# Attention of the later token tiles spread over the expert heads, one tile at a time

## The chip, the cores and the metric

The kernel runs on one core of a Trainium2 chip. The metric is the device time of one execution in microseconds. Engines: TensorE (PE), VectorE (DVE), ScalarE (ACT), GpSimd (POOL) and SyncE (SP). Each runs its own instructions in order and waits for the others on semaphores; 16 DMA engines move data for all of them. SP issues the plain loads and stores, POOL the gathers.

## What is computed

Two transformer blocks over 512 tokens of width 1024, all in float32. The first block (windowed attention with a context, a convolution branch, and a mixture of experts) isn't touched. The second, cut to what matters:

```python
fox_out = forgetting_attention(...)      # 8 heads of 64, causal softmax with a decay
sb_out = stick_breaking_attention(...)   # 8 heads of 64, causal, sigmoids and a reversed cumsum
mixed = concat([rms_norm(fox_out, g_out_fox), rms_norm(sb_out, g_out_sb)], -1)
x = x + gt1 * (mixed @ w_out)                        # w_out: 1024 x 1024, 4 MiB
h2 = rms_norm(x, g_norm_ffn) * (1 + sc2) + sh2
query = (h2 @ w_query).reshape(t, 8, 2, 128)         # w_query: 1024 x 2048, 8 MiB
# peer layer: per head, top 16 of 128 x 128 experts by two halves of the query
u, v = expert_down[experts], expert_up[experts]      # one row of 1024 each
x = x + gt2 * sum(gelu(h2 . u) * gate * v)
return rms_norm(x, g_final)
```

## The kernel before

Tokens are worked in TT = 4 tiles of 128 (P). The second block ends with 32 expert heads, numbered n: head n is expert head n % 8 of token tile n // 8. A head has PARTS = 8 parts, written out by hand on every engine, and each part takes two of the head's 16 expert choices. For a choice, POOL gathers, for the 128 token and expert-slot pairs, a row of 8 KB (the expert's down and up vectors) into one of the pair buffers, 1 MiB in all. VectorE takes the dot product with h2 (`dot`), ScalarE the gelu and scales the gates (`coefs`), TensorE adds the up rows into banks 4 and 5 or 6 and 7 (`up_sums`, one part later). Then the buffer is free and POOL may gather the next choice. Gather m uses buffer m modulo 8 in tile 0 (m < FIRST = 128) and eleven buffers after that: the three others lie in storage that the attention uses until then. In the same parts VectorE finds the top 16 of head n + 2 (`topk_part`).

Before the expert heads, tile 0 alone is attended, and its queries are made. The attention of tiles 1 to 3 (24 units of stick-breaking and 24 of forgetting attention, a unit being one head of one tile, with 256, 384 or 512 keys) is done in steps. Step k of a kind works on unit k and, some steps later, on its follow-up, so the engines have units in flight (`stick_step`, `fox_step`). The first LEAD = 6 steps run ahead of head 0. The others, then the norm (`out_norm`), the turning, the product with w_out in three pairs of blocks, the three `second_norm`s and the first two query heads are dealt out over the first FRONT = 6 expert heads by the table PLAN. In each part the engine does its `peer_part` and then `attend` for the steps of that part. The other six query heads (`query_b`) follow at the ends of heads 6 to 11. Each query head is a product with 256 columns of w_query, loaded by SP as a piece of 1 MiB, for the 384 tokens of all three tiles.

ScalarE has one set of activation functions loaded at a time. `coefs` needs gelu, the attention exp and log, and a switch is an instruction of its own (ACT_TABLE_LOAD).

At a tile's edge h2 is repeated in another order on TensorE and ScalarE (`repeat_rows`, `repeat_out`), the sums of the tile are closed (`edge`), and a tile's final norm (`last_norm`) is made in head 6 of the next tile.

## Time and profile before

| | |
|---|---|
| median of 3 runs | 2968.79 us (2963.34 to 2986.03) |
| profiled execution | 2979.64 us, its span 2977.9 us |
| mean granted TensorE clock | 0.87 |
| busy: TensorE, VectorE, ScalarE, POOL | 2268.4, 1421.2, 759.3, 597.2 us |
| moved by DMA | 922.19 MB, of these 559.01 MB in POOL's queue |

The page gives each engine's busy time, 40 slices of the span, the DMA queues, the chain that ended last, and the costliest groups of instructions. A slice is 74.4 us. The expert heads begin at about 1510 us, in slice 20 counted from 0. Busy times on TensorE and VectorE are of instructions that overlap little or not at all; the share of the DMA engines can be full at 421 GB/s.

### The profile page before, as it was taken

How to read it: one execution, taken by the hardware profiler on the slowest of the kernel's cores; microseconds unless marked ns; L12 is line 12 of the kernel's file. 1: busy time of each engine (PE TensorE's matmuls, PEld its weight loads, DVE VectorE, ACT ScalarE, POOL GpSimd, SP SyncE). 2: the span in 40 equal slices, each digit the busy share in tenths (PEclk: the TensorE clock that was granted, in tenths of full speed). 3: DMA queues.
4: the chain of work that ended last, by engine and by line, in shares of the span. 5: the costliest groups of instructions: out<-in, count | busy, mean ns of one | idle time of the engine just before them, and what ended most of it. 6: DMA issues, size and time to landing. Idle time of an engine off the chain costs nothing. (4 is left out here: it accounts for less than half of the span.)

```text
span 2977.9 us, 28985 instructions
## 1 busy us (share of the span) xinstructions
PE 2268.4 (76%) x9828; PEld 972.8 (33%) x9828; DVE 1421.2 (48%) x3332; ACT 759.3 (25%) x1753; POOL 597.2 (20%) x590
## 2 busy tenths in 40 slices
PE   5997899887777776799988978877765655465554
PEld 2543444432222222655655443322211111111110
DVE  2575401420000001401377667657678777777765
ACT  2104301110000001412177653222222212222212
POOL 0000000010000000000112223344344434344432
PEclk9999999989988988799999889889877777887877
DMA  9268429489999998312347868899999999999996
GB/s 338 60 242 290 164 81 216 189 308 405 400 403 397 396 395 327 114 57 85 138 175 288 305 261 319 361 391 416 417 420 422 421 421 422 420 407 421 422 421 253
DMA packets 211725, 922.19 MB, mean 310 GB/s; under 512 B 18986, under 2 KB 58968, under 8 KB 119694
## 3 DMA queue, kind: packets, MB, share of 16 engines
q0 software_dynamic: 80448, 559.01, 46.3%
q1 hardware_dynamic: 121360, 352.86, 32.4%
q10 hardware_dynamic: 9790, 8.73, 0.9%
q8 instruction: 66, 1.08, 0.1%
q14 instruction: 61, 0.50, 0.0%
HBM read 888.78 MB, written 31.77 MB: 309 GB/s over the span
## 5 line engine op out<-in xcount | busy, mean ns | idle before, releaser
L2604 PE MATMUL bank<-ring,arena_w 128*32 128x512 f32 x1568 | 593.9, 777 | 316.9 <-ACT arena_w L1327 316.6
L894 POOL DMA_INDIRECT ring<-in_expert_pair,ids x392 | 419.4, 1070 | 1037.3 <-PE bank L2604 658.9
L1978 PE MATMUL bank<-arena_h,ring 128*128 128x128 f32 (+2 forms) x1264 | 365.3, 450 | 5.6 <-ACT arena_h L1132 3.2
L2258 PE MATMUL bank<-ring,arena_h 128*64 128x512 f32 x1056 | 278.8, 688 | 85.7 <-DMA ring<-in_w_exp_up 80.8
L2604 PEld LDWEIGHTS bank<-ring,arena_w 128*32 128x32 f32 x1568 | 103.1, 127 | 653.4 <-ACT arena_w L1327 469.3
L1927 DVE CUSTOM_DVE_ANT_0 ring<-ring,arena_h 128x1024 f32<-128x1024 f32 x203 | 245.1, 1225 | 82.2 <-DMA ring<-in_expert_pair,ids 47.4
L1927 DVE CUSTOM_DVE_ANT_0 ring<-ring 128x1024 f32<-128x1024 f32 x189 | 229.6, 1225 | 80.1 <-DMA ring<-in_expert_pair,ids 71.8
L1978 PEld LDWEIGHTS bank<-arena_h,ring 128*128 128x128 f32 x1264 | 206.1, 198 | 155.6 <-issue 119.0
L1325 ACT ACTIVATE arena_w<-arena_w 128x2 f32<-128x2 f32 x256 | 51.9, 203 | 770.7 <-DVE arena_w L1927 770.3
L1650 DVE TENSOR_TENSOR arena_q<-arena_q,bank 128x256 f32<-128x256 f32 x32 | 13.5, 421 | 487.9 <-ACT arena_q L1069 487.9
L2258 PEld LDWEIGHTS bank<-ring,arena_h 128*64 128x64 f32 x1056 | 95.9, 157 | 266.1 <-issue 260.6
L2604 PE MATMUL bank<-arena_h,arena_w 128*32 128x512 f32 x200 | 128.7, 779 | 31.3 <-ACT arena_w L1327 31.3
L1327 ACT ACTIVATE arena_w<-arena_w 128x32 f32<-128x32 f32 x512 | 136.4, 313 | 8.4
L2271 PE MATMUL bank<-ring,arena_q 128*64 128x512 f32 x528 | 120.6, 598 | 19.9 <-DVE arena_q L1653 19.3
L2604 PE MATMUL bank<-pair_last,arena_w 128*32 128x512 f32 x140 | 97.6, 838 | 43.3 <-ACT arena_w L1327 43.3
L2604 PE MATMUL bank<-arena_v,arena_w 128*32 128x512 f32 x140 | 93.4, 804 | 28.6 <-ACT arena_w L1327 28.4
L860 POOL DMA_DIRECT2D ring<-in_w_in x3 | 2.7, 908 | 536.0 <-PE bank L2271 536.0
L1069 ACT ACTIVATE arena_q<-bank 128x256 f32<-128x256 f32 x32 | 12.3, 384 | 327.2 <-PE bank L2258 327.2
L1325 ACT ACT_TABLE_LOAD x63 | 80.8, 1283 | 50.7 <-DVE arena_w L1927 49.9
L1464 DVE SCALAR_TENSOR_TENSOR arena_x<-arena_x,convc 128x512 f32<-128x512 f32 x120 | 90.2, 752 | 4.3
L1984 PE MATMUL bank<-ring,arena_h 128*128 128x512 f32 x192 | 86.4, 606 | 0.0
L1984 PE MATMUL bank<-ring,arena_q 128*128 128x512 f32 x176 | 80.3, 614 | 4.8 <-DVE arena_q L1535 4.8
(473 smaller groups left out, 2982.8 us busy)
## 6 DMA issues: line engine op xcount, KB each, us to landing
ring<-in_w_exp_gate SPq DMA_DIRECT2D x33, 2048.0 KB, 20.2
ring<-in_w_exp_up SPq DMA_DIRECT2D x33, 2048.0 KB, 24.7
...
```

Of the source, the lines that this page charges most:

```text
L894: pool.indirect_dma_start(pair[pair_of(m)], None, A["expert_pair_2"], bass.IndirectOffsetOnAxis(ap=ids[n % 2][:, r:r + 1], axis=0)).then_i ...
L1069: act.activation(silu_g[b], bank[2 + b][:, 0:256], ACT.Silu).then_inc(silu_done, 1)
L1325: link(act.activation(gel[:, k0:k0 + count], dots[:, k0:k0 + count], ACT.Gelu))
L1327: act.activation(sel_q[:, n % 2, k, :], sel_q[:, n % 2, k, :], ACT.Copy, scale=gel[:, k:k + 1]).then_inc(sel_done, 1)
L1464: link(dve.scalar_tensor_tensor(out=conv[:, cc, :], in0=u_pad[:, cc, k:k + T], scalar=convc[:, cc, k:k + 1], in1=conv[:, cc, :], op0=ALU.m ...
L1650: dve.tensor_tensor(hid[b], silu_g[b], bank[2 + b][:, 256:512], ALU.mult).then_inc(hid_done, 1)
L1927: dve.tensor_tensor_reduce(buf, buf, h2_q[r % 4], 1.0, 0.0, ALU.mult, ALU.add, dots[:, r:r + 1]).then_inc(dots_done, 1)
L1978: mm = pe.matmul(dst, w[:, c, at], rhs[:, c, :], start=(c == 0), stop=(c == chunks - 1))
L1984: mm = pe.matmul(dst, xT[:, c, t * P:(t + 1) * P], w[:, c, at], start=(c == 0), stop=(c == chunks - 1))
L2258: mm = pe.matmul(bank[2 + b][at, :].rearrange("p (g f) -> p g f", g=2), xbT[b][:, c, :], gu[:, :, c, 256 * half:256 * half + 256], start=( ...
L2271: mm = pe.matmul(bank[6 + b][CAP * j:CAP * j + CAP, :], hidT[b][:, k, CAP * half:CAP * half + CAP], slab(n)[:, half, k, 512 * j:512 * j + ...
L2604: mm = pe.matmul(bank[4 + 2 * (n // H % 2) + half][at, :], sel_q[:, n % 2, k0 + j, :], pair[pair_of(m + j)][:, D + 512 * half:D + 512 * ha ...
```

## The change

Tiles 1, 2 and 3 are attended one at a time: tile t + 1 during the 8 expert heads of tile t. A plan for a tile (`planned`) deals the 25 attention steps (for tile 1 the 19 that are left after the lead) over the first 30 of the tile's 64 parts, and fixes the parts of the rest: `out_norm` at 30, the turning at 31, the two blocks of w_out at 32 and 36, `second_T` at 39, the eight query heads at 41, 44, 48, 51, 54, 57, 60 and 62. w_out comes in four and w_query in eight pieces of 1 MiB per tile, through the two halves of one buffer (`hold_a`), so both are loaded for each of the three tiles; a query head now multiplies 128 tokens. The shift row of `second_norm` is loaded anew for each tile, since it shares its place with `mixed`. The eight buffers of tile 0 serve until the last tile (FIRST = 384), and the eleven only there. The expert sums always use banks 4 and 5, so the part 1 of a tile waits on TensorE for `last_add` of the tile before. The three final norms move to heads 1, 3 and 5 of the last tile. ScalarE loads the exp and log functions after `coefs` in each part that has an attention step.

The diff, cut to its core:

```diff
...
-        pair += [hold_a[:, 2 * D:4 * D], arena_v[:, 6144:6144 + 2 * D], pair_last[:, :]]
-        FIRST = H * K16
+        pair += [arena_v[:, 2 * D * i:2 * D * i + 2 * D] for i in range(1, 4)]
+        FIRST = (TT - 1) * H * K16
...
-        def wq_b_of(h):
-            if h == 1:
-                return wq_b[1], slab_in[slot2(S_WQ)], loaded2(S_WQ) + 16
-            return wq_b[0], slab_in[slot2(S_FOX + 2)], loaded2(S_FOX + 2) + 16 * max(1, h)
+        PIECES = 4 + H
+        def piece(t, i):
+            at = hold_a[:, 2 * D * (i % 2):2 * D * (i % 2) + 2 * D]
+            turn = 16 * ((t - 1) * PIECES // 2 + i // 2 + 1)
+            there = (slab_in[slot2(S_WQ)], loaded2(S_WQ) + turn) if i % 2 == 0 else (wo_b_in, turn)
+            if i < 4:
+                return at.rearrange("p (c n) -> p c n", c=4), there, cols_cp(A["w_out_2"], i // 2)[:, 4 * (i % 2):4 * (i % 2) + 4, :]
+            h = i - 4
+            return (at.rearrange("p (c n) -> p c n", c=DC), there,
+                    A["w_query_2"][:, h * 2 * P:(h + 1) * 2 * P].rearrange("(p c) n -> p c n", c=DC))
+        def wo_used(t, q):
+            return 2 * TT + 2 + 4 * (t - 1) + q + 1
+        def wq_used(t, h):
+            return 4 + H * (t - 1) + h + 1
...
-            return (n, 0, 0) if n < H else ((n - H) // NT[1], 1 + (n - H) % NT[1], 1)
+            return n % H, n // H, min(1, n // H)
...
-        LAST_AT = 6
+        LAST_AT = (1, 3, 5)
...
-            return first <= n < (H if first == 0 else UNITS)
+            return first <= n < first + H
...
+        ST_FOX = H + OUTS[1]
+        ST_NORM = ST_FOX + H + FOX_OUT[1]
+        ST_TURN, ST_OUT, ST_COLS, ST_QUERY = ST_NORM + 1, ST_NORM + 2, ST_NORM + 4, ST_NORM + 5
         PARTS = 8
         LEAD = 6
-        PLAN = [[[s for s in range(LEAD, STEPS) if int(sum(weight[LEAD:s]) / sum(weight[LEAD:]) * (FRONT * PARTS - 1)) == h * PARTS + p]
-                 for p in range(PARTS)] for h in range(H)]
+        ATTEND_PARTS = 30
+        LATER = {ST_NORM: 30, ST_TURN: 31, ST_OUT: 32, ST_OUT + 1: 36, ST_COLS: 39}
+        LATER.update({ST_QUERY + h: at for h, at in enumerate((41, 44, 48, 51, 54, 57, 60, 62))})
+        def planned(t):
+            first = LEAD if t == 1 else 0
+            plan = [[[] for p in range(PARTS)] for h in range(H)]
+            for k in range(first, ST_NORM):
+                at = (k - first) * ATTEND_PARTS // (ST_NORM - first)
+                plan[at // PARTS][at % PARTS].append(k)
+            for k, at in LATER.items():
+                plan[at // PARTS][at % PARTS].append(k)
+            return plan
+        PLAN = [parts for t in range(1, TT) for parts in planned(t)]
...
-            sp.wait_ge(sbo_pe, UNITS)
-            for j in range(2):
-                sp.dma_start(wo_b[j], cols_cp(A["w_out_2"], j)).then_inc(wo_b_in, 16)
-            sp.wait_ge(o_done, H * TT + UNITS)
-            load_rows(1)
-            for h in range(H):
-                dst, there, _ = wq_b_of(h)
-                if h == 0:
-                    sp.wait_ge(wo_pe, 4 * TT)
-                elif h == 1:
-                    sp.wait_ge(h2_done, 2 * TT)
-                else:
-                    sp.wait_ge(q_pe, 4 + 2 * (h if h > 2 else 1))
-                sp.dma_start(dst, A["w_query_2"][:, h * 2 * P:(h + 1) * 2 * P].rearrange("(p c) n -> p c n", c=DC)).then_inc(there, 16)
-            sp.wait_ge(q_pe, 4 + 2 * H)
-            for dst, src in ((gt2_2, mod2_d[0, 5 * D:6 * D]), (gfin, A["g_final_2"])):
-                sp.dma_start(dst, src.partition_broadcast(P)).then_inc(rows2_in, 16)
+            sp.wait_ge(q_pe, 2)
+            sp.wait_ge(o_done, H * TT + H)
+            load_halves(rows_2[1][0], 2 * D)
+            load_row(rows_2[1][1], mod2_d[0, 4 * D:5 * D])
+            load_row(rows_2[1][3], A["g_norm_ffn_2"])
+            for t in range(1, TT):
+                sp.wait_ge(o_done, H * TT + (t + 1) * H)
+                for i in range(PIECES):
+                    dst, (there, _), src = piece(t, i)
+                    if 2 <= i < 6:
+                        sp.wait_ge(wo_pe, wo_used(t, i - 2))
+                    elif i >= 6:
+                        sp.wait_ge(q_pe, wq_used(t, i - 6))
+                    sp.dma_start(dst, src).then_inc(there, 16)
+                    if i == 1:
+                        sp.wait_ge(attT_pe, 2 * t + 2)
+                        load_row(rows_2[1][2], mod2_d[0, 3 * D:4 * D])
+                        if t == 1:
+                            load_halves(gt2_2, 5 * D)
+            load_row(gfin, A["g_final_2"])
             for t in range(TT):
                 sp.wait_ge(fin_done, t + 1)
...
                         pool.wait_ge(q_pe, m - 1)
                     if m == FIRST:
-                        pool.wait_ge(wo_pe, 4 * TT)
-                        pool.wait_ge(q_pe, 4 + 2 * 2)
-                        pool.wait_ge(qh_done, H)
...
+            def query_out_b(t, h):
+                act.wait_ge(q_pe, wq_used(t, h))
+                link(act.activation(qT2[:, h, :], bank[1 + h % 3][:, 0:2 * P], ACT.Copy), q_done)
+            def attend(t, s):
                 if s < ST_FOX:
-                    stick_step(H + s, H)
+                    if s == 0 and t >= 2:
+                        act.wait_ge(q_pe, wq_used(t - 1, H - 1))
+                    stick_step(H * t + s, H * t)
                 elif s < ST_NORM:
-                    fox_step(H + s - ST_FOX, H)
+                    fox_step(H * t + s - ST_FOX, H * t)
                 elif s == ST_NORM:
-                    out_norm(1)
-                elif s < ST_OUT:
-                    for k in range(DC):
-                        act.wait_ge(attT_pe, 2 + k + 1)
-                        link(act.activation(mixT2[1][:, k, :], bank[(1, 2, 3, 6, 7)[k % 5]][:, 0:3 * P], ACT.Copy,
-                                            scale=gob[:, k // AC:k // AC + 1]), attT_done)
-                elif s < ST_QUERY:
-                    t = s - ST_OUT
-                    if 1 <= t < TT:
-                        second_norm(t, 1, rows_2[1][3])
-                    for u in {4: (1,), 5: (2, 3)}.get(t, ()):
-                        second_columns(u, 1, h2T_2[1][:, :, (u - 1) * P:u * P], H2T_BANKS[u])
-                else:
-                    query_out_b(s - ST_QUERY)
+                    out_norm(t)
+                elif s == ST_TURN:
+                    turned_out(t)
+                elif s == ST_OUT + 1:
+                    second_norm(t, 1, h2r_2[t])
+                elif s == ST_COLS:
+                    second_columns(t, 1, h2T_2[1], H2T_BANKS[1])
+                elif s >= ST_QUERY:
+                    query_out_b(t, s - ST_QUERY)
...
-                if n < H and PLAN[n][part]:
-                    if any(s < ST_FOX for parts in PLAN[n:] for steps in parts for s in steps):
-                        act.preload_act_table_set(EXP_LN)
+                if n < len(PLAN) and any(s < ST_NORM for s in PLAN[n][part]):
+                    act.preload_act_table_set(EXP_LN)
...
-            def attend(s):
+            def attend(t, s):
                 if s < ST_FOX:
-                    stick_step(H + s, H)
+                    stick_step(H * t + s, H * t)
                 elif s < ST_NORM:
-                    fox_step(H + s - ST_FOX, H)
+                    fox_step(H * t + s - ST_FOX, H * t)
                 elif s == ST_NORM:
-                    out_norm(1)
-                elif 1 <= s - ST_OUT < TT:
-                    t = s - ST_OUT
                     if t == 1:
                         norm_gain(1)
-                    second_norm(t, 1, *rows_2[1][0:3], h2r_2[t], tmp_2[1], WO_BANKS[t])
+                    out_norm(t)
+                elif s == ST_OUT + 1:
+                    second_norm(t, 1, *rows_2[1][0:3], h2r_2[t], tmp_2[1], WO_BANKS[1], (rows2_in, 16 * (10 + t)))
...
-            def last_norm(t):
+            def last_add(t):
+                dve.wait_ge(peer_done, t + 1)
                 for j in range(2):
                     at = slice(512 * j, 512 * j + 512)
-                    dve.wait_ge(peer_done, t + 1)
-                    link(dve.tensor_tensor(tmp_p, bank[4 + 2 * (t % 2) + j][:, :], gt2_2[:, at], ALU.mult))
+                    link(dve.tensor_tensor(tmp_p, bank[4 + j][:, :], gt2_2[j], ALU.mult))
                     link(dve.tensor_tensor(xr[:, t, at], xr[:, t, at], tmp_p, ALU.add), fin_add if j == 1 else None)
+            def last_norm(t):
                 one = slice(t, t + 1)
                 dve.wait_ge(ssq_done, SQ_LAST + t + 1)
                 link(dve.tensor_scalar(rms_t[:, one], ssq[:, one], 1.0 / D, EPS, ALU.mult, ALU.add), ms_done)
...
-            def query_b(h, halves=(0, 1)):
-                w, there, count = wq_b_of(h)
-                pe.wait_ge(there, count)
-                for half in halves:
-                    m = 2 * h + half
-                    if m >= 3:
-                        pe.wait_ge(q_done, 4 + m - 2)
-                    project(bank[1 + m % 3][:, 0:3 * P], w, slice(half * P, (half + 1) * P), h2T_2[1]).then_inc(q_pe, 1)
-            def attend(s):
+            def query_b(t, h):
+                w, there, _ = piece(t, 4 + h)
+                pe.wait_ge(*there)
+                if h >= 3:
+                    pe.wait_ge(q_done, wq_used(t, h - 3))
+                for half in range(2):
+                    mm = project(bank[1 + h % 3][:, half * P:(half + 1) * P], w, slice(half * P, (half + 1) * P), h2T_2[1])
+                mm.then_inc(q_pe, 1)
+            def attended_b(t, j):
+                for half in range(2):
+                    w, there, _ = piece(t, 2 * j + half)
+                    pe.wait_ge(*there)
+                    for c in range(4):
+                        mm = pe.matmul(bank[WO_BANKS[1][j]][:, :], mixT2[1][:, 4 * half + c, :], w[:, c, :],
+                                       start=(half == 0 and c == 0), stop=(half == 1 and c == 3))
+                    mm.then_inc(wo_pe, 1)
...
-                    if s == 0:
+                    if s == 0 and t == 1:
                         pe.wait_ge(q_done, 4)
                         pe.wait_ge(proj_out, 18 + PROJS)
-                    stick_step(H + s, H)
+                    if s == 0 and t >= 2:
+                        pe.wait_ge(q_done, wq_used(t - 1, H - 1))
+                        pe.wait_ge(rep_done, 8 * t)
...
-                        second_T(1, 1, h2r_2[1], H2T_BANKS[1])
-                    if t == TT + 1:
-                        pe.wait_ge(res_done, 2 * (TT + 3) + 2)
-                        second_T(2, 1, h2r_2[2], H2T_BANKS[2])
-                    if t == TT + 2:
-                        pe.wait_ge(h2T_done, 2 * (TT + 1) + 2)
-                        second_T(3, 1, h2r_2[3], H2T_BANKS[3])
+                    fox_step(H * t + s - ST_FOX, H * t)
+                elif s == ST_TURN:
+                    turned(t)
+                elif ST_OUT <= s < ST_OUT + 2:
+                    if s == ST_OUT:
+                        pe.wait_ge(attT_done, 2 * t + 2)
+                    attended_b(t, s - ST_OUT)
+                elif s == ST_COLS:
+                    second_T(t, 1, h2r_2[t], H2T_BANKS[1])
                 elif s >= ST_QUERY:
                     if s == ST_QUERY:
-                        pe.wait_ge(h2T_done, 4 * TT)
-                    query_b(s - ST_QUERY)
+                        pe.wait_ge(h2T_done, 2 * (TT + t) + 2)
+                    query_b(t, s - ST_QUERY)
...
+                if part == 1 and n % H == 0 and n > 0:
+                    pe.wait_ge(fin_add, n // H)
+                    edge(True)
                 if part >= 1:
...
             pe.wait_ge(rep_done, 8)
             for s in range(LEAD):
-                attend(s)
+                attend(1, s)
             for n in range(TT * H):
                 t = n // H
                 if n % H == 0 and t > 0:
-                    if t == 1:
-                        pe.wait_ge(q_done, 4 + 2 * (n - FRONT + 2))
+                    pe.wait_ge(q_done, wq_used(t, H - 1))
                     repeat_rows(t, range(3))
                 if n > 0:
                     up_sums(n - 1, K16 - 2, 2)
                 if n % H == 0 and t > 0:
+                    edge(False).then_inc(peer_done, 1)
                     repeat_rows(t, range(3, 8))
-                    edge(t - 1, False).then_inc(peer_done, 1)
-                    if t >= 2:
-                        pe.wait_ge(fin_add, t - 1)
-                    edge(t, True)
                 if n > 0 and n + 2 < TT * H:
                     peer_scores(n + 2)
                 for part in range(PARTS):
                     peer_part(n, part)
-                    for s in PLAN[n][part] if n < H else ():
-                        attend(s)
+                    for s in PLAN[n][part] if n < len(PLAN) else ():
+                        attend(t + 1, s)
                     if n == 0 and part == 0:
                         spread(1)
                         peer_scores(2)
-                if FRONT + AHEAD - 1 <= n + 1 < FRONT + H - 1:
-                    if n == H:
-                        pe.wait_ge(rep_done, 8 * 2)
-                    query_b(n + 1 - FRONT + 1)
             up_sums(TT * H - 1, K16 - 2, 2)
-            edge(TT - 1, False).then_inc(peer_done, 1)
+            edge(False).then_inc(peer_done, 1)
...
```

## Rows read from the trace of the kernel before

**Rows 1.** The page's 40 slices, 74.4 us each: DMA busy tenths, GB/s
```profile
DMA  9268429489999998312347868899999999999996
GB/s 338 60 242 290 164 81 216 189 308 405 400 403 397 396 395 327 114 57 85 138 175 288 305 261 319 361 391 416 417 420 422 421 421 422 420 407 421 422 421 253
```

**Rows 2.** Stretches: PE, PEld, DVE, ACT, POOL busy (count), granted clock, DMA share, GB/s
```profile
1521.00:1957.00 436.00, 371.75 (x1706) 182.21 (x1704) 309.48 (x745) 228.30 (x456) 123.30 (x120) 0.86 0.79 306
1957.00:2300.00 343.00, 228.38 (x1036) 71.58 (x1032) 245.67 (x604) 86.00 (x256) 147.73 (x131) 0.82 1.01 415
2340.00:2920.00 580.00, 333.27 (x1490) 73.73 (x1490) 429.73 (x1032) 135.64 (x424) 246.13 (x231) 0.79 1.01 419
2360.00:2590.00 230.00, 130.09 (x544) 27.85 (x546) 173.99 (x430) 52.63 (x167) 97.32 (x92) 0.79 1.01 421
1521.00:1630.00 109.00, 96.81 (x555) 61.95 (x552) 93.19 (x218) 89.53 (x154) 31.70 (x30) 0.92 0.71 266
```

**Rows 3.** The DMA view, 1900 to 2160 us: queues and query loads
```profile
q0 software_dynamic: 13882, 101.08, 94.1%
q1 hardware_dynamic: 5228, 5.36, 6.2%
...
ring<-in_w_query SPq DMA_DIRECT2D x5, 1024.0 KB, 22.4
```

**Rows 4.** All eight query loads, from issue to landing
```profile
DMA to landing us min/median/max: 6.0/14.9/26.9
```

**Rows 5.** Stretches of 10 us, columns as in rows 2
```profile
1920.00:1930.00 10.00, 10.00 (x58) 4.95 (x59) 6.86 (x15) 1.14 (x4) 4.01 (x4) 0.78 1.01 421
1930.00:1940.00 10.00, 9.14 (x43) 4.06 (x41) 4.15 (x12) 2.25 (x9) 2.03 (x3) 1.00 0.99 375
1940.00:1950.00 10.00, 3.63 (x8) 0.55 (x8) 7.01 (x19) 1.42 (x6) 5.64 (x6) 0.57 0.99 394
...
1990.00:2000.00 10.00, 6.03 (x32) 2.27 (x32) 7.41 (x24) 1.78 (x8) 3.86 (x3) 0.97 0.76 282
```

**Rows 6.** TensorE in order of time: start, duration, what
```profile
1476.57 7.31 PE L1978 MATMUL bank<-arena_h,ring 128*128 128x128 f32 x64
...
1515.26 1.12 PE L2453 MATMUL bank<-ring,later_neg 128*128 128x512 f32 x2 [0.84 <-DVE ring L1738]
...
1517.74 1.00 PE L2469 MATMUL bank<-arena_v,ring 128*128 128x64 f32 x8
...
1520.60 1.91 PE L2604 MATMUL bank<-ring,arena_w 128*32 128x512 f32 x8
1522.44 1.16 PE L2445 MATMUL bank<-arena_v 64*128 64x128 f32 x8
...
1782.14 7.13 PE L1984 MATMUL bank<-arena_v,arena_q 128*128 128x512 f32 x16
```

**Rows 7.** Groups by line and shape, 1510 to 1760 us
```profile
L1188 ACT ACTIVATE ring<-ring,ones 128x512 f32<-128x512 f32 x7 | 5.1, 723 | 0.2
...
L1738 DVE TENSOR_TENSOR ring<-ring,before 128x128 f32<-128x128 f32 x19 | 5.5, 292 | 0.7
...
L1735 DVE SCALAR_TENSOR_TENSOR ring<-bank,ring 128x512 f32<-128x512 f32 x7 | 4.8, 691 | 1.9 <-ACT ring L1188 1.7
...
L1745 DVE TENSOR_TENSOR ring<-bank,ring 128x256 f32<-128x256 f32 x7 | 3.0, 423 | 3.3 <-PE bank L2457 2.9
```

**Rows 8.** ScalarE in order of time
```profile
1869.42 1.28 ACT L1320 ACT_TABLE_LOAD   x1
1870.71 0.21 ACT L1320 ACTIVATE arena_w<-arena_w 128x16 f32<-128x16 f32 x1
```

**Rows 9.** VectorE in order of time: first and last of one second_norm
```profile
1796.52 0.69 DVE L1545 TENSOR_TENSOR ring<-bank,arena_v 128x512 f32<-128x512 f32 x1
...
1804.79 1.23 DVE L1553 TENSOR_TENSOR ring<-ring,arena_v 128x1024 f32<-128x1024 f32 x1
```

**Rows 10.** Waits, 1960 to 2340 us: total, times, longest
```profile
DVE ring L1927 <- ACT arena_h L1334: 20.4, 2, 15.8
```

249 lines of the change are left out of this document (104 added, 145 removed).

## The prediction

> **What bounds the kernel now.** I read the page in slices first, for where the DMA engines are full and where they are not [rows 1]. Slices 20 to 26, counted from 0, move 175 to 391 GB/s; from slice 27 on it is 416 to 422 with one dip, up to the last. So the expert heads of tiles 1 to 3 are bound by the gathers, and those of tile 0, which carry the whole attention of the other three tiles, by something else. Then the busy times by stretch [rows 2]. A gather is 128 rows of 8 KB, 1.049 MB, and at 421 GB/s takes 2.49 us. From 1957 us on the chip keeps to it (231 gathers in 580 us, 2.51 each). Before that, 1521 to 1957 us, 120 gathers take 436 us, 3.63 each, at 306 GB/s, while TensorE is busy 371.8 of 436 us. In the part with stick-breaking attention (1521 to 1630 us) three engines are nearly full: TensorE 96.8, VectorE 93.2, ScalarE 89.5 of 109 us. The reader should see that the time lost is DMA time, 436 x (421 - 306)/421 = 119 us, and that engines lose it. I then went to single instructions for what the engines do per pair of gathers [rows 6, 7], and to the weight loads in the DMA view [rows 3, 4], since the change buys the 119 us with more of these.
>
> **Removed.** The front's excess: at best tile 0 becomes bound by DMA, -119 us. The next two tiles lose in the trace of before 343 x 6/421 = 5 us (415 GB/s instead of 421 [rows 2]); they are rebuilt too, so these go to the credit: -124.
>
> **Added transfers.** w_out (4 MiB) and w_query (8 MiB) are read for each of three tiles instead of once: 24 MiB more, 25.2 MB, at 421 GB/s 60 us. The shift row is read three times instead of once: 1.05 MB, 2.5 us. Query pieces have runs of 1 KB (1025 bytes a packet against 7281 for gathers [rows 3]); in the stretch with five of them the rate is 415. If all of its 5 us were theirs it would be 1 us a piece, if none 0; I take 0.5 for the 24 pieces that the new stretch holds, 12 us (0 to 24). Sum with no stall anywhere: -124 + 60 + 2.5 + 12 = -49 us. As the total is now DMA-bound everywhere, this is the ceiling of the gain; with free query pieces -61.
>
> **What the attention costs inside a DMA-bound head.** A pair of gathers (one part of a head) takes 4.98 us of DMA. Engines need for it, from 2360 to 2590 us (92 gathers, 46 pairs), TensorE 2.8, VectorE 3.8, ScalarE 1.1 us [rows 2]; VectorE's gaps between dependent instructions add some 0.4 (an estimate: a third of its 1.2 us of idle time), 4.2. The plan puts 25 steps (19 for the first tile) in 30 parts. A stick unit of 512 columns costs TensorE 1.16 + 3.48 = 4.6 us at full clock, a pair's sums 1.9 [rows 6]; VectorE three operations of 0.69 and one of 0.3, with gaps 2.5 us; for 256 columns 0.42 each, 1.7 [rows 7]. Eight units take 13 steps, at 1.2 parts a step 15.6 parts: VectorE 4.2 + 8 x 2.5/15.6 = 5.5 us per part for the last tile, 5.3 for the middle one (2.1 a unit), 5.0 for the first. Over 4.98 that is 8 us, 4 us, 0. TensorE stays below: 1.9 + 0.5 x 4.6 = 4.2 at the full 2.4 GHz, 4.9 at the front's granted 0.86 of it (a mean of that level and 1.2 GHz, with the engine busy 85% of the time). Engines that are all near full hold each other up: from 1521 to 1630 us a pair took 7.3 us where the busiest engine had 6.45, 12% more. At lower load I take a third of it over 30 parts, 6 us for each of three tiles (bounds 0 and 18): 18. Sum 30 us.
>
> **The serial steps.** Eight gather buffers hold 20 us of transfers, of which a part in work needs about half. What a stop costs is in the trace: with eight buffers, a query block of 10.6 us on TensorE (in 1920 to 1940 us) left rates of 421, 375 and 394, in sum 1.7 us of DMA [rows 5]. So the new blocks of 7.1 us (attended_b, half of w_out) and 3.7 us (a query head, 7.3 for two [rows 6]) cost nothing in themselves; with the cover gone they would cost themselves, 24 x 3.7 + 6 x 7.1 = 131 us. second_norm is 9.5 us on VectorE's in-order queue [rows 9], and the dots of the next pair, their ScalarE scaling, TensorE's sums and so the next gathers wait behind it; with the wait for TensorE's block some 14 us, 4 beyond the cover. out_norm is shorter. 3 us a tile, 9 (0 to 20). At a tile's edge VectorE waited 15.8 us for the repeated rows and the DMA lost 3.3 us in the worst 10 us [rows 5, 10]; the new edge has no 10.6 us block beside it, but TensorE now waits at part 1 for last_add (banks 4 and 5 are shared), behind which all its sums are queued. I keep 3 us for two edges, 6 (0 to 15).
>
> **Weights that come late.** SP issues a piece only when one of two halves is free, and the query steps stand 3 parts apart (6 gathers and a piece, 7.34 MB, 17.4 us). Under full gathers a piece of 1 MiB landed after 22.4 us, at the least load after 6.0 [rows 3, 4]. TensorE waits in order, sums behind it, gathers behind these. But while it waits the DMA works on gathers and piece alike. At 1.05 MB/22.4 us the piece has 47 GB/s and the gathers 374, for 16.8 us, the piece has 0.79 MB by then, and 0.26 MB at 1.05 MB/6.0 us add 1.5: 18.3 instead of 17.4. At 24 steps 21 us; some steps are 4 parts apart, so I take half, 10 (0 to 34). The arbitration that this rests on is a rule of the Trainium skill too ("DMA: Bandwidth & Descriptors", Queues, rings and completion order): each engine takes whole packets from its queues in turn. By that rule small packets against large ones get a small share, which agrees with the 22.4 us; it speaks against re-reading weights under gathers, and is the mechanism of the second rival.
>
> The w_out pieces are the same case: 0 and 1 are issued when the last fox unit is out (part 28) and wanted at part 32, 20 us later, 2 and 3 wanted 4 parts after the first are used; their runs are 2 KB. They are in the 10.
>
> **Moved for nothing.** sqT and fqT are stored by tile, in copies of the same size. The lead of six steps is all 256 wide: up to 5 us earlier, against as much of ramp; 0. The three final norms come in the last tile, with eleven buffers: 8 output rows' worth of DMA there instead of 4, and one edge; +2. SP's output stores now stand behind all pieces, and nobody waits for them before the end. Behind SP's new wait for the turned rows (attT_pe) stand only the shift row, which VectorE wants five parts later, and pieces that have no free half yet. POOL's one wait at the first gather of tile 3 is for attention that ended a tile's half ago. ScalarE's and TensorE's waits at a tile's first step are for queries that the preceding part has brought.
>
> **Sum.** -49 + 30 + 9 + 6 + 10 + 2 = +8 us; as coinciding stalls hide one another, I take off a tenth of the 55 us of stalls: +3. The profiled execution took 2979.64 us (span 2977.9), 10.9 above the median of three, so a difference is what carries over: 2982.6 beside it, 2968.8 + 3 = 2972 as median.
>
> **Rivals.** First, the gain arrives: the late weights are work for the DMA engines and cost nothing, and the coupling is 0, so 12 + 3 + 3 + 2 = 20 remain of the stalls, and -49 + 20 = -29, or with cheap query pieces -41: 2934. For it: the 10.6 us block that cost 1.7. Against: VectorE alone needs 5.3 to 5.5 us a part in two tiles.
> Second, slower: TensorE's waits for query pieces, parts 41 to 62. If all eight gathers have landed when a piece comes, the DMA engines stand for the 3.7 us block and the first sums (1.9), 5.6 us less what the next piece covers; at 2.5 us on average, 24 steps, +60 - 10 = +53: 3022, and at the full 5.6 +127: 3096. It decides from the point at which a piece lands later than 17.4 us after its slot came free. For it: 22.4 us. Against: the queue is then less full, and 6.0 us were seen. Less than nothing it can't cost: no step starts before its piece.
> Third, the engines' coupling stays at the front's 12% for 30 parts of three tiles (54 us instead of 18): +39, 3008.
> Fourth, ScalarE's table switches. Each part with a step switches to the exp/log set and back, 69 parts, 138 loads of 1.28 us; the load is followed by its activation with no gap (1869.42 + 1.28, next at 1870.71 [rows 8]). In the 15.6 parts of a 512 wide stick stretch ScalarE then has 26 loads (33 us), four activations of some 0.65 us a unit (0.72 the longest [rows 7]; 21 us) and 0.9 a part for the scaling (14 us), 4.4 us a part. If a switch cost twice its 1.28 us it would be 6.5 (6.0 in the narrowest tile), 1.3 above the DMA over 90 parts, 117 us in place of the 30 above: +90, 3059. For it speaks a page only, against it the row. The page is "ScalarE: Activation LUTs" of the Trainium skill, What ACT_TABLE_LOAD costs: it adds a drain of about 1.38 us to each load. By that rule the kernel would be clearly slower; the trace shows no such time.
> Fifth, the change doesn't do what it says: tile 0 stays at over 3 us a gather because the granted clock falls, the new bytes are paid and half of the 119 returns: +60, 3030.
>
> **How the numbers follow.** Forecast, within 1%: 0.44. Gain arrives: 0.26, of which 0.22 beyond 1%. Late weights: 0.14. Coupling: 0.08, half of it beyond 1%. Table switches 0.04, first tile not freed 0.04. So faster by over 1% 0.22; slower 0.14 + 0.04 + 0.04 + 0.04 = 0.26; within 0.52. 1%, 30 us, is about what this kernel's measurement can tell from no change (its three runs span 23 us). The range leaves out the upper half of the late weights, the table switches and the deepest gains: 2925 to 3030.
>
> **What would show it.** Right: from about 1530 us on 405 to 421 GB/s through three tiles; the gather of tile 1's start near 1870 instead of 1957, that of tile 3's start within 20 us of before; VectorE busy 75 to 90% in all three. Dips at the norms and the edges, of under 5 us each. Late weights: waits of TensorE for query DMAs of over 3 us, with the rate under 380 in the second half of each tile. Coupling: rate under 390 in the first half of the second and third. I would be wrong outright if buffers drained at every part, or if the small packets cost much more DMA time than 0.5 us a piece.

## The result and the profile after

| | before | after |
|---|---|---|
| median | 2968.24 us (4 runs) | 3020.2 us (2998.02 to 3037.1, 4 runs) |
| ratio, 95% interval | | 1.0168 [1.0136, 1.02] |
| profiled execution, its span | 2979.64, 2977.9 us | 2998.02, 2996.2 us |
| moved by DMA | 922.19 MB | 948.46 MB |

The change makes the kernel 1.7% slower. The profiled execution after is the fastest of its four, so the two profiles are only 18 us apart. First the page after: slices (as [rows 1]) and the two large queues.

```profile
GB/s 336 59 247 289 155 87 221 183 323 405 406 400 399 399 394 306 85 56 85 190 319 419 388 359 410 292 400 416 387 410 316 388 401 363 411 395 421 422 422 298
...
q0 software_dynamic: 80448, 559.01, 46.1%
q1 hardware_dynamic: 142832, 379.08, 34.6%
```

Slices 20 to 26, counted from 0, rose from 175 to 391 GB/s to 292 to 419, as the change wanted. But slices 28 to 35, full before with one dip, now fall to 316, 363 and 387. The stretches say the same; columns as in [rows 2], and each of the first three is about one tile's heads:

```profile
1500.00:1880.00 380.00, 250.40 (x1246) 105.57 (x1245) 262.78 (x646) 137.57 (x319) 135.10 (x124) 0.80 0.94 379
1880.00:2260.00 380.00, 274.43 (x1446) 121.16 (x1446) 274.73 (x667) 170.46 (x360) 135.01 (x128) 0.85 0.97 381
2260.00:2640.00 380.00, 281.81 (x1511) 130.68 (x1511) 272.34 (x654) 175.00 (x357) 138.27 (x130) 0.87 0.96 379
2640.00:2900.00 260.00, 156.86 (x758) 40.58 (x756) 194.74 (x479) 70.74 (x202) 114.59 (x101) 0.77 1.00 415
```

Three tiles in a row stay at 380 GB/s, no engine above 75% busy: they are bound by DMA, with holes. Where are the holes? Five stretches hold most of them: around the two w_out blocks of tiles 0, 1 and 2, and around the ends of tiles 0 and 1.

```profile
1700.00:1760.00 60.00, 37.59 (x193) 15.94 (x191) 34.57 (x84) 13.63 (x37) 16.61 (x16) 0.83 0.82 315
2100.00:2140.00 40.00, 25.11 (x141) 10.32 (x141) 29.96 (x71) 12.66 (x33) 11.40 (x12) 0.79 0.96 370
2500.00:2540.00 40.00, 29.04 (x172) 13.37 (x172) 30.81 (x76) 10.50 (x33) 15.39 (x15) 0.81 0.84 325
1860.00:1920.00 60.00, 43.55 (x265) 22.06 (x264) 33.28 (x80) 30.50 (x57) 16.94 (x16) 0.91 0.77 296
2240.00:2340.00 100.00, 83.69 (x492) 45.40 (x493) 73.48 (x167) 61.75 (x109) 30.32 (x29) 0.91 0.86 324
```

Against 421 GB/s the three w_out stretches lose 60 x 106/421 + 40 x 51/421 + 40 x 96/421 = 29 us, and the two ends 18 + 23 = 41 us. In a second profile of the same kernel (after_again) the same five stretches carry 356, 357, 364, 334 and 326 GB/s and lose 21 and 35 us, so a single trace gives these sums only roughly. The worst of them, in order of time: SyncE's issues of pieces, and TensorE's w_out blocks in tile 0.

```profile
1646.05 0.94 SPq L786 DMA_DIRECT2D ring<-in_w_out  x2
...
1676.76 3.82 SPq L786 DMA_DIRECT2D ring<-in_w_out  x2
1701.84 13.20 SPq L786 DMA_DIRECT2D ring<-in_w_query  x2
```

```profile
1696.72 5.08 PE L2556 MATMUL bank<-ring 128*128 128x512 f32 x8 [2.79 <-DMA ring<-in_w_out]
1708.39 6.07 PE L2556 MATMUL bank<-ring 128*128 128x512 f32 x8 [6.59 <-DMA ring<-in_w_out]
```

Pieces 2 and 3, issued from 1676.76, are not there at 1701.8, 25 us later. TensorE stands 6.59 us, VectorE's `second_norm` behind it, the dots behind that, and the eight gather buffers stay full. VectorE waits 15.12 us for the second block, and POOL issues no gather for 20.17 us:

```profile
1714.57 0.69 DVE L1558 TENSOR_TENSOR ring<-bank,arena_q 128x512 f32<-128x512 f32 x1 [15.12 <-PE bank L2556]
```

```profile
1717.09 0.94 POOL L919 DMA_INDIRECT ring<-in_expert_pair,ids  x1 [20.17 <-PE bank L2611]
```

From 1700 to 1760 us the chip issues 16 gathers, against 21 in e6_free below, with the same packets. TensorE's waits for pieces in the three tiles:

```profile
PE bank L1994 <- DMA ring<-in_w_query: 36.4, 9, 7.7
PE bank L2556 <- DMA ring<-in_w_out: 16.5, 4, 6.6
```

Nine waits of 24 query steps, and four at w_out: fewer than the prediction's second rival had them, and longer.

### The profile page after: what moved, and what is told of

The parts are those of the page before. It is cut to its first block, busy times and chain, and to the rows that moved or that the text cites. A ratio compares the mean times of both kernels' runs of the same rounds, so it can differ in the third digit from the quotient of the medians.

```text
span 2996.2 us, 30146 instructions
## 1 busy us (share of the span) xinstructions
PE 2276.9 (76%) x10340; PEld 1025.6 (34%) x10340; DVE 1421.4 (47%) x3340; ACT 843.0 (28%) x1824; POOL 603.0 (20%) x590
## 2 busy tenths in 40 slices
DMA packets 233201, 948.46 MB, mean 317 GB/s; under 512 B 19466, under 2 KB 75832, under 8 KB 141166
## 4 chain that ended last, share of the span: by engine, by line
PE 40%; DMA 34%; DVE 16%; issue 5%; ACT 4%; POOL 1%; SPq 0%; another core or an unknown queue 0%; DVEq 0%; ACTq 0%; POOLq 0%
PE bank L1994 16%; DMA ring<-in_w_exp_up 12%; DMA ring<-in_expert_pair,ids 10%; DVE ring L1941 6%; DMA ring<-in_w_query 6%; PE bank L2274 5%; PE bank L2000 5%; PE bank L2611 5%; DMA ring<-in_w_out 2%; DMA arena_h<-in_expert_pair,ids 1%; PE bank L2556 1%; DMA ring<-in_w_mod 1%; PE bank L2013 1%; ACT L1346 1%; DVE arena_h L1941 1%
## 5 line engine op out<-in xcount | busy, mean ns | idle before, releaser
L2611 PE MATMUL bank<-ring,arena_w 128*32 128x512 f32 x1668 | 574.4, 747 | 348.3 <-ACT arena_w L1348 345.3
L919 POOL DMA_INDIRECT ring<-in_expert_pair,ids x417 | 457.5, 1097 | 1131.0 <-PE bank L2611 749.2
L1941 DVE CUSTOM_DVE_ANT_0 ring<-ring,arena_h 128x1024 f32<-128x1024 f32 x232 | 279.4, 1224 | 103.6 <-DMA ring<-in_expert_pair,ids 79.7
L1665 DVE TENSOR_TENSOR arena_q<-arena_q,bank 128x256 f32<-128x256 f32 x32 | 13.5, 421 | 481.0 <-ACT arena_q L1094 481.0
L2611 PE MATMUL bank<-arena_h,arena_w 128*32 128x512 f32 x236 | 142.3, 735 | 13.8 <-ACT arena_w L1348 13.8
L1346 ACT ACT_TABLE_LOAD x94 | 120.6, 1283 | 93.1 <-DVE arena_w L1941 92.2
L1994 PE MATMUL bank<-ring 128*128 128x128 f32 x768 | 115.8, 322 | 36.4 <-DMA ring<-in_w_query 36.4
L2287 PE MATMUL bank<-ring,arena_q 128*64 128x512 f32 x528 | 120.6, 598 | 20.0 <-DVE arena_q L1668 19.4
L1994 PEld LDWEIGHTS bank<-ring 128*128 128x128 f32 x768 | 111.7, 235 | 65.8 <-DMA ring<-in_w_query 51.8
```

Of the source, the lines that this page charges most:

```text
L919: pool.indirect_dma_start(pair[pair_of(m)], None, A["expert_pair_2"], bass.IndirectOffsetOnAxis(ap=ids[n % 2][:, r:r + 1], axis=0)).then_i ...
L1346: link(act.activation(gel[:, k0:k0 + count], dots[:, k0:k0 + count], ACT.Gelu))
L1941: dve.tensor_tensor_reduce(buf, buf, h2_q[r % 4], 1.0, 0.0, ALU.mult, ALU.add, dots[:, r:r + 1]).then_inc(dots_done, 1)
L1994: mm = pe.matmul(dst, w[:, c, at], rhs[:, c, :], start=(c == 0), stop=(c == chunks - 1))
L2287: mm = pe.matmul(bank[6 + b][CAP * j:CAP * j + CAP, :], hidT[b][:, k, CAP * half:CAP * half + CAP], slab(n)[:, half, k, 512 * j:512 * j + ...
L2611: mm = pe.matmul(bank[4 + half][at, :], sel_q[:, n % 2, k0 + j, :], pair[pair_of(m + j)][:, D + 512 * half:D + 512 * half + 512], start=Fa ...
```

## The experiments

The table gives each kernel's median, its ratio to the kernel before on the same chip with its interval, and what it changes. Differences between kernels of different comparisons are taken between ratios.

| kernel | us | ratio [95%] | what |
|---|---|---|---|
| after_again | 3010.89 | 1.0127 [1.009, 1.0164] | the changed kernel |
| e1_cut_pieces | 2895.1 | 0.9712 [0.9663, 0.9761] | pieces of one eighth |
| e2_wide_runs | 2950.05 | 0.9927 [0.9904, 0.995] | same bytes, 8 KB runs |
| e3_narrow | 2994.86 | 1.009 [1.006, 1.0121] | attention 256 wide |
| e4_no_wait | 3008.59 | 1.0111 [1.007, 1.0153] | pieces not waited for until the tile's end |
| e6_free | 2970.64 | 1.0016 [0.999, 1.0042] | the same, and issued early |
| e5_before_eight | 2975.8 | 1.0005 [0.998, 1.0029] | before, eight buffers in tiles 1 and 2 |
| e7_no_gelu | 3000.33 | 1.0107 [1.006, 1.0153] | Gelu replaced |
| c_pairs | 2976.4 | 1.0009 [0.9982, 1.0036] | query pieces in 2 KB runs |
| c_long | 2958.75 | 0.9947 [0.9923, 0.997] | all pieces in 4 KB runs |
| c_shift | 2962.79 | 0.9976 [0.9952, 1.0] | c_long, attention over 34 parts |
| c_mid | 2952.62 | 0.9927 [0.9906, 0.9949] | c_long, attention over 32 parts |

**The changed kernel again.** 

> The changed kernel once more, to see its spread beside the others and to have a second profile. Both theories: 1.01 to 1.02 of before, 2998 to 3037 us.

42 us above before (2969.41): the slowdown is real, 1.3 to 1.7%.

**Pieces: bytes or runs?** e1_cut_pieces (the w_out and w_query products of tiles 1 to 3 are then made of what lay in the buffer):

```diff
-                    sp.dma_start(dst, src).then_inc(there, 16)
+                    at8 = slice(0, 256)
+                    sp.dma_start(dst[:, 0:1, at8], src[:, 0:1, at8]).then_inc(there, 16)
```

> The changed kernel, but each of the 36 weight pieces loads an eighth of its 1 MiB (the rest of the piece is what lay there, so queries and attention output of tiles 1 to 3 are wrong). Every wait stays. 33 MB less are moved, 78 us at 421 GB/s. Theory A (late pieces: the DMA engines stand idle around the steps that wait for a piece): 78 + 12 for small packets + 25 to 40 for lateness, some 115 to 130 us faster than the changed kernel, 2890 to 2905, 0.97 to 0.98 of before. Theory B (the engines' coupling in the attention parts loses the time, lateness nothing): 78 to 90 us faster, 2930 to 2942.

e2_wide_runs loads other rows, whole, into the same halves (so TensorE multiplies with other weights):

```diff
-                    sp.dma_start(dst, src).then_inc(there, 16)
+                    flat = hold_a[:, 2 * D * (i % 2):2 * D * (i % 2) + 2 * D]
+                    if i < 4:
+                        src = A["w_out_2"][256 * i:256 * i + 256, :].rearrange("(p r) n -> p (r n)", r=2)
+                    else:
+                        src = A["w_query_2"][P * (i - 4):P * (i - 3), :]
+                    sp.dma_start(flat, src).then_inc(there, 16)
```

> The changed kernel, each piece still 1 MiB but read in runs of 8 KB instead of 1 or 2 KB (other elements of the same weights, so the numbers of tiles 1 to 3 are wrong). Theory A, with the small share of small packets as the reason for the lateness: a piece lands in 8 to 12 us under full load instead of over 20, 35 to 50 us faster than the changed kernel. Theory B: 5 to 12 us faster, from the packets alone.

The pieces' DMAs from issue to landing, first in the changed kernel (after_again), then with 8 KB runs; the last figure of the longer rows is the median:

```profile
DMA to landing us min/median/max: 7.4/26.9/38.2
ring<-in_w_query SPq DMA_DIRECT2D x24, 1024.0 KB, 29.0
ring<-in_w_out SPq DMA_DIRECT2D x12, 1024.0 KB, 19.0
```

```profile
DMA to landing us min/median/max: 8.7/9.4/13.8
ring<-in_w_query SPq DMA_DIRECT2D x24, 1024.0 KB, 9.3
ring<-in_w_out SPq DMA_DIRECT2D x12, 1024.0 KB, 9.5
```

e1_cut_pieces lies in theory A's range, and e2_wide_runs gains more than its 35 to 50 us. The same megabyte lands in a third of the time, and the kernel gains 61 us (3010.89 - 2950.05). The landing time falls with the length of the runs: 29.0 us with 1 KB, 19.0 with 2 KB, 9.3 and 9.5 with 8 KB. The bytes cost too: e1_cut_pieces moves 33 MB less than e2_wide_runs, 78 us at 421 GB/s, and is 55 us faster (64 by the ratios, give or take 16). But these bytes were in the prediction's sum. What it missed is the shape of the pieces, and that alone turns the gain of e2_wide_runs, 0.7%, into a loss of 1.3%.

**How wide is the attention's share?** e3_narrow gives tiles 2 and 3 the attention of tile 1:

```diff
-            return n % H, n // H, min(1, n // H)
+            return n % H, min(1, n // H), min(1, n // H)
```

> The changed kernel, but the attention of tiles 2 and 3 is that of tile 1, 256 keys wide (its numbers are wrong there); all steps, waits and loads stay. Theory B (three engines near full hold each other up at 384 and 512 keys): 25 to 40 us faster than the changed kernel, no stretch below 400 GB/s in the first half of tiles 1 and 2. Theory A: under 10 us faster.

16 us by the medians, 0.37% (11 us) with 0.48% of uncertainty between the ratios. That meets neither theory's figure and can't be told from nothing: it doesn't show what the width costs.

**Late, or merely small?** Small runs could cost in two ways: TensorE waits, or the queue carries less. In e4_no_wait TensorE multiplies with another resident array; the products of tiles 1 to 3 are left out in effect, the loads stay.

```diff
+                    if i >= 2:
+                        sp.wait_ge(*piece(t, i - 2)[1])
...
-                w, there, _ = piece(t, 4 + h)
-                pe.wait_ge(*there)
+                w = skT[:, 0:DC, :]
+                if h == H - 1:
+                    for i in (PIECES - 2, PIECES - 1):
+                        pe.wait_ge(*piece(t, i)[1])
...
-                    w, there, _ = piece(t, 2 * j + half)
-                    pe.wait_ge(*there)
+                    w = view(arena_w, 0, 4, 512)
```

> The changed kernel with all its 36 pieces loaded as they are (same bytes, same 1 KB and 2 KB runs, nearly the same moments), but TensorE multiplies with another resident array in their place and waits for the pieces only once per tile, before their place in the buffer is used again. It leaves the second block's w_out and w_query products of tiles 1 to 3 out. Theory A (what costs is that the pieces arrive after they are wanted, and everything queued on TensorE, ScalarE and VectorE stands): most of what the long runs gave comes back here too, 2950 to 2970 against 3010.9 for the changed kernel. Rival B (what costs is the queue's lower rate while small packets pass, and the bytes themselves; the waits are covered): within 12 us of the changed kernel, 2999 to 3015.

3008.59: taken alone, this spoke for rival B. The trace says otherwise. Two stretches of e4_no_wait, and a wait of its TensorE (line 1996 is the last query head, which waits for the last two pieces of the tile; the profile names no releaser):

```profile
1720.00:1740.00 20.00, 16.50 (x110) 7.62 (x112) 15.78 (x38) 5.53 (x19) 8.98 (x8) 0.80 1.03 404
1880.00:1900.00 20.00, 18.89 (x146) 7.04 (x144) 10.86 (x26) 11.97 (x23) 4.55 (x5) 1.00 0.56 211
...
```

```profile
PE bank L1996 <- issue: 30.9, 2, 16.5
```

The hole at w_out is gone, but the lateness had only moved to the tile's end: I had left a wait there, and the last piece still came late. So e6_free issues each piece as soon as its half's last one has landed, instead of after its use:

```diff
-                    if 2 <= i < 6:
-                        sp.wait_ge(wo_pe, wo_used(t, i - 2))
-                    elif i >= 6:
-                        sp.wait_ge(q_pe, wq_used(t, i - 6))
+                    if i >= 2:
+                        sp.wait_ge(*piece(t, i - 2)[1])
```

> As e4_no_wait (TensorE multiplies with another resident array, the second block's w_out and w_query products of tiles 1 to 3 are left out), but the queue of the pieces is no longer paced by their use either: each piece is issued as soon as the one before it in its half of the buffer has landed, so that all twelve of a tile are there long before the one wait at its end, where e4_no_wait still stood 14 and 16 us. Same bytes, same 1 KB and 2 KB runs. Theory A (lateness costs): the stalls of the w_out steps and of the tiles' ends are gone, 2950 to 2975 against 3010.9 for the changed kernel. Rival B (small packets lower the rate whether they are waited for or not): 2995 to 3015.

2970.64. The five stretches of before in this kernel, and one more of query pieces:

```profile
1700.00:1760.00 60.00, 36.10 (x220) 14.49 (x220) 42.97 (x100) 16.95 (x45) 23.28 (x21) 0.83 1.03 408
2100.00:2140.00 40.00, 26.27 (x156) 12.55 (x156) 28.97 (x72) 10.29 (x30) 18.61 (x15) 0.84 1.02 411
2500.00:2540.00 40.00, 26.72 (x156) 12.42 (x156) 25.57 (x62) 9.10 (x28) 16.86 (x16) 0.83 1.03 411
1860.00:1920.00 60.00, 50.35 (x276) 24.92 (x271) 47.91 (x109) 43.93 (x78) 19.36 (x19) 0.91 0.84 320
2240.00:2340.00 100.00, 87.11 (x473) 42.26 (x469) 82.74 (x187) 73.71 (x122) 33.05 (x32) 0.93 0.88 340
...
1740.00:1860.00 120.00, 81.23 (x510) 40.92 (x508) 76.54 (x183) 27.73 (x83) 47.79 (x40) 0.87 1.02 410
```

The w_out stretches lose 4 us instead of 29, the ends 14 + 19 = 33 instead of 41. That is 33 us less (19 less when set against after_again's profile). The ratios give 1.0127 - 1.0016 = 1.1%, 33 us (give or take 13). TensorE still waits at the last query head of a tile, but 8.8 us in three times where e4_no_wait had 30.9 in two. What stays of the 61 us, 0.9% or 26 us (give or take 10), is then small packets without lateness. The last row fits that: with small packets passing the DMA engines are full (1.02) and carry 410. The same stretch of e2_wide_runs:

```profile
1740.00:1860.00 120.00, 78.17 (x460) 38.70 (x462) 81.01 (x199) 27.38 (x84) 47.03 (x42) 0.84 1.01 421
```

In the three tiles such packets pass for some 600 us; 600 x 11/421 = 16 of the 26 us, by this estimate. The other 10 are within the error.

**Fewer buffers.** e5_before_eight is the kernel before with this part of the change alone:

```diff
-        FIRST = H * K16
+        FIRST = (TT - 1) * H * K16
```

> The kernel before with one part of the change alone: eight gather buffers until the last tile, where it had eleven from tile 1 on. If the prediction's tiles 1 and 2 are right in holding the queue full (415 to 419 GB/s) with less cover, this costs under 8 us (2965 to 2977 against 2969). Rival: the three buffers fewer, some 8 us of stock less for every stall, are what uncovers the coupling, and cost 15 to 40 us alone (2985 to 3010).

```profile
2340.00:2920.00 580.00, 338.43 (x1492) 72.59 (x1492) 428.25 (x1029) 135.17 (x423) 255.94 (x234) 0.77 1.01 418
1960.00:2300.00 340.00, 223.96 (x985) 68.79 (x983) 241.16 (x589) 84.50 (x250) 136.25 (x125) 0.81 0.99 404
```

Tile 1 carries 404 GB/s, 415 before, and the rest as much as before [rows 2]. The whole costs 1.5 us by the ratio, with an interval of -6 to +9: in the kernel before, the three buffers are not it. Whether eleven would have covered the late pieces in the changed kernel isn't shown; there the attention holds their storage.

**Table switches.** e7_no_gelu replaces the experts' activation by one that needs no table of its own:

```diff
-                link(act.activation(gel[:, k0:k0 + count], dots[:, k0:k0 + count], ACT.Gelu))
+                link(act.activation(gel[:, k0:k0 + count], dots[:, k0:k0 + count], ACT.Square))
```

> The changed kernel with the experts' Gelu replaced by Square, which needs no other table of ScalarE: the 163 table loads of 1.28 us (209 us of ScalarE) go, nearly all. This changes the values of the output, not the work. Fourth rival (table switches lie on the chain dot, coefficient, multiplication, free buffer): 2960 to 2985 against 3010.9. Against it: ScalarE is idle half of every tile and the loads are covered: within 10 us of the changed kernel.

I had the count wrong: the 94 loads ahead of the Gelu went, but the preload of the exp set, 69 times, stayed. The page's groups of after, then of e7_no_gelu:

```profile
L1346 ACT ACT_TABLE_LOAD x94 | 120.6, 1283 | 93.1 <-DVE arena_w L1941 92.2
...
L1367 ACT ACT_TABLE_LOAD x69 | 88.5, 1283 | 1.2
```

```profile
L1367 ACT ACT_TABLE_LOAD x69 | 88.5, 1283 | 1.2
```

120.6 us less on ScalarE change the ratio from 1.0127 to 1.0107, 0.2% with an uncertainty of 0.6% (6 us, give or take 18): nothing that can be told from noise.

**Mending the runs.** c_pairs loads query weights for two heads and half of the rows (2 KB runs), accumulates over two pieces, and changes nothing at w_out:

```diff
-            return (at.rearrange("p (c n) -> p c n", c=DC), there,
-                    A["w_query_2"][:, h * 2 * P:(h + 1) * 2 * P].rearrange("(p c) n -> p c n", c=DC))
+            return (at.rearrange("p (c n) -> p c n", c=DC // HEADS), there,
+                    A["w_query_2"].rearrange("(p c) n -> p c n", c=DC)[:, DC // HEADS * k:DC // HEADS * (k + 1),
+                                                                      2 * P * HEADS * g:2 * P * HEADS * (g + 1)])
```

> The changed kernel with the query weights loaded for pairs of heads and half of the rows at a time: as many pieces, as many bytes, at the same parts of the plan, with runs of 2 KB in place of 1 KB; the w_out pieces stay at 2 KB. Correct result. Theory A (the size of the runs sets how late a piece lands): query pieces land in about 15 us in place of 27, and the time falls by 20 to 40, to 2970 to 2990. Rival (the long runs of the earlier experiment gained by w_out's pieces, which stand at the one place where everything waits): within 10 us of the changed kernel.

Its TensorE has no wait for a query piece left, and as many at w_out as before, where the first stretch still has its hole. How long the query pieces took to land is not in its trace:

```profile
PE bank L2570 <- DMA ring<-in_w_out: 16.8, 4, 6.3
```

```profile
1700.00:1760.00 60.00, 36.66 (x186) 16.24 (x184) 33.67 (x79) 12.65 (x34) 16.40 (x16) 0.81 0.82 312
```

c_long has HEADS = 4 in the same lines, and w_out as two chunks of rows by all columns:

```diff
+                return (at.rearrange("p (c n) -> p c n", c=2), there,
+                        A["w_out_2"].rearrange("(c p) n -> p c n", p=P)[:, 2 * i:2 * i + 2, :])
...
-        LATER.update({ST_QUERY + h: at for h, at in enumerate((41, 44, 48, 51, 54, 57, 60, 62))})
+        LATER.update({ST_QUERY + h: at for h, at in enumerate((41, 43, 45, 47, 51, 54, 58, 62))})
```

> The changed kernel with 4 KB runs for both kinds of pieces: w_out two chunks of rows by all 1024 columns, the query weights two chunks by the columns of four heads, each product accumulated over four pieces; the last query pieces of each half stand at parts 47 and 62. Same bytes, same number of pieces. Correct result. Theory A: pieces land in about 12 us, and the time is 2945 to 2970, up to 60 below the changed kernel and up to 20 below the kernel before. Rival: accumulating over four pieces brings all the waits forward to parts 41 to 47, in which VectorE is full, and half of the gain is lost: 2975 to 2995.

1.2% (35 us, give or take 14) came back with the query pieces alone, another 0.6% with c_long, which makes the runs of both kinds 4 KB and also moves six query steps; how much of that is w_out's isn't separated. No matmul waits for a piece any more (the loads of weights into TensorE wait 3.3 us, in two times). What holes remain lie mostly at the tiles' starts, where VectorE is 87% busy (69.70 of 80 us, below). c_shift thins the attention there:

```diff
-        ATTEND_PARTS = 30
-        LATER = {ST_NORM: 30, ST_TURN: 31, ST_OUT: 32, ST_OUT + 1: 36, ST_COLS: 39}
+        ATTEND_PARTS = 34
+        LATER = {ST_NORM: 34, ST_TURN: 35, ST_OUT: 36, ST_OUT + 1: 39, ST_COLS: 42}
...
-                at = (k - first) * ATTEND_PARTS // (ST_NORM - first)
+                weight = [3] * (ST_FOX - first) + [2] * (ST_NORM - ST_FOX)
+                at = sum(weight[:k - first]) * ATTEND_PARTS // sum(weight)
```

> c_long (4 KB runs) with the attention's steps spread over 34 parts in place of 30, and the wide steps of the first branch given 3 shares to the second's 2, so that VectorE has about one step in 1.6 parts at the start of a tile, where c_long's rate was 300 to 340 GB/s for some 80 us; the last query pieces stand at parts 47 and 60. Correct result. If those dips are VectorE's coupling (dots, top-k and attention in one part), they shrink by half: 2935 to 2950 against 2958.75. Rival: the later norms and pieces crowd the middle of the tile and give it back: 2952 to 2970.

c_mid has 32 parts, w_out at 35 and 39, `second_T` at 41, query pieces at 43, 44, 46, 47, 51, 54, 57 and 60.

> c_long with the attention spread over 32 parts (wide steps 3 shares, the others 2, as in c_shift, where the tile's start rose from 316 to 341 GB/s to 354 to 420), and four parts between the two w_out steps as in c_long, one more part ahead of the first (c_shift had three between and fell to 322 GB/s there). Correct result. If both dips are separate and each keeps its better form: 2945 to 2953, below both kernels. Rival: the steps pushed into parts 41 to 47 take it back: 2955 to 2965.

The start of tile 1 and the w_out steps of tile 0 in c_long, in c_shift and in c_mid:

```profile
1880.00:1960.00 80.00, 61.11 (x309) 30.18 (x309) 69.70 (x171) 58.72 (x102) 30.94 (x28) 0.89 0.90 338
1700.00:1780.00 80.00, 54.18 (x320) 26.36 (x318) 51.98 (x123) 19.75 (x54) 26.90 (x24) 0.83 0.99 400
```

```profile
1880.00:1960.00 80.00, 60.43 (x324) 27.38 (x321) 72.02 (x170) 51.32 (x98) 31.73 (x31) 0.88 0.98 382
1700.00:1780.00 80.00, 55.16 (x325) 27.77 (x323) 46.45 (x107) 17.71 (x47) 26.84 (x24) 0.85 0.92 372
```

```profile
1880.00:1960.00 80.00, 62.09 (x332) 29.05 (x330) 70.77 (x172) 54.23 (x100) 32.03 (x30) 0.87 0.94 371
1700.00:1780.00 80.00, 52.09 (x324) 25.87 (x316) 49.44 (x116) 20.78 (x54) 29.13 (x26) 0.87 0.95 387
```

Thinning the attention helps the start (338 to 382 GB/s), but the stretch of w_out falls from 400 to 372, so c_shift gains nothing on c_long. Its two w_out steps stand three parts apart instead of four, and there the late pieces are back. In c_long TensorE's matmuls had no such wait, in c_shift they have:

```profile
PE bank L2574 <- DMA ring<-in_w_out: 14.8, 5, 3.6
```

c_mid, between the two, is 0.7% faster than the kernel before and 2% faster than the changed one. Against c_long it is 0.2% with an uncertainty of 0.3%: that last step isn't shown.

## Why the prediction was right and where it was not

It said 2972, within 2925 to 3030; the kernel takes 3011 to 3020. That is inside the range, near its upper end, but not within the 1% of no change that was the forecast. The term that was sized wrong is "Weights that come late", and the small packets with it; both mechanisms were named.

| term of the sum | predicted | measured |
|---|---|---|
| everything but small packets and late weights | -19 | -19 (e2 against before; -22 by the ratio) |
| small packets | 12 | 26, of which 16 seen in the rate |
| late weights | 10, less a tenth | 33 (e6 to after) |

The -19 is -124 + 60 + 2.5, nine tenths of 30 + 9 + 6, and 2.

**Removed, added, coupling, serial steps, edges.** Their sum is right within the uncertainty of 7 us, and e2_wide_runs is the kernel that shows it. Whether each is right isn't shown by the sum, and in part it may be luck. By the same terms e1_cut_pieces should lie at -19 - 78 = -97 us, since it loads an eighth of 36 MiB. It lies at -74 (-86 by the ratio, give or take 15). With these bytes gone its tiles carry 372 to 393 GB/s, not 421, so a saved byte is not worth its full time there, or a stall was larger than I had it.

The first tile was freed. Tile 1's first gather, the 129th of all, was issued at 1957.02 us in the kernel before, and here at 1863.46; I had said 1870. That of tile 3 came 17 us after its old place (2634.80 and 2618.20), within the 20 I had given:

```profile
1863.46 1.90 POOL L919 DMA_INDIRECT ring<-in_expert_pair,ids  x1 [8.41 <-PE bank L2611]
```

For the coupling, the first halves of tiles 1 and 2 tell more than e3_narrow. First the changed kernel, then e2_wide_runs:

```profile
1880.00:2070.00 190.00, 149.09 (x818) 63.07 (x818) 152.62 (x369) 129.55 (x238) 66.27 (x66) 0.89 0.93 367
2250.00:2440.00 190.00, 159.56 (x880) 73.07 (x878) 149.16 (x351) 131.57 (x232) 68.72 (x66) 0.95 0.92 360
```

```profile
1880.00:2070.00 190.00, 140.87 (x716) 61.20 (x711) 154.49 (x380) 119.29 (x223) 73.69 (x70) 0.89 0.98 391
2250.00:2440.00 190.00, 151.07 (x776) 67.24 (x772) 155.26 (x371) 123.25 (x220) 71.20 (x68) 0.92 0.96 380
```

With long runs these halves lose 13.5 + 18.5 = 32 us against 421 GB/s, where the prediction had 24 of coupling and 6 for the two edges; in the changed kernel they lose 24 + 28 = 52. So in this trace the coupling and the edges were there about as predicted, and late pieces came on top of them. e3_narrow adds little: 12 of the 30 us were the width of tiles 2 and 3, and its 16 is not told apart from 0 or from 12.

**Eight buffers cover a stop.** Right as far as it went (e5_before_eight, +1.5), and in the old kernel a 10.6 us block cost 1.7 us [rows 5]. But it was applied to steps one at a time. At w_out the stops come in one chain: wait, block, wait of 6.6 us, block, `second_norm`. 20 us of cover don't hold that: POOL stood 20.17 us.

**Weights that come late.** Three faults. I let a piece that is late cost only its excess over the schedule, since DMA works on while TensorE waits; but gathers stop once eight are there. I sized it by the query pieces' pace in their middle (18.3 us a piece; e4_no_wait's issues are 127.8 us apart over seven, 18.3) and not at the two places where no other work is queued: w_out's second pair, asked for only after the first is used, and the last piece ahead of the next tile. And I took 22.4 us for a landing where the query pieces' median was 29.0 and the longest of all 38.2. By the stretches 25 of the 33 us lie at w_out (17 with after_again's profile), which the prediction waved through in one sentence ("They are in the 10"). The query pieces weigh as much in all, if their small packets are counted too: c_pairs gets 35 us back and leaves the waits at w_out as they are.

**The rule of the Trainium skill.** The landing times fit what the prediction cited: under the same gathers a piece takes 29.0 us in runs of 1 KB, 19.0 in runs of 2 KB and 9.3 to 9.5 in runs of 8 KB. "DMA: Bandwidth & Descriptors" of the Trainium skill (Queues, rings and completion order) states the rule that each engine takes whole packets from its queues in turn. A small packet would then get a small share beside large ones, and the three landing times agree; the order in which packets were served is in no trace. I had read it as a reason for lateness, and should have seen in it the cure: longer runs.

**Rivals.** The second (late pieces, 3022) has the right mechanism and nearly the time; its place was half wrong, since it spoke of 24 query steps. The first (2934) needs the pieces on time: e2_wide_runs, where they are, is at 2950. The third would put 24 us more into the two first halves above, 54 instead of 30, and 32 were measured. The fourth is excluded: of its 138 loads the 69 ahead of the Gelu are gone in e7_no_gelu, worth half of its 90 us, and the kernel moved 6, give or take 18. The fifth is excluded by the 129th gather, 94 us earlier than before though twelve pieces pass in that tile too.

**What would show it.** "405 to 421 GB/s through three tiles" was wrong (379 to 381), VectorE at 75 to 90% too (69 to 72%, since it stood). The mark of late weights was there in part: waits for query pieces of up to 7.7 us, but in the second halves of the tiles a rate under 380 only in tile 0 (373; 401 and 391 after it). The mark of coupling, under 390 in the first halves of tiles 1 and 2, was there too (367 and 360).
